# Latent attention in a three-block transformer stack: both first maxima and exponentials of a head ahead of its divides, and the next head's key copied behind the fourth divide

## What is computed

```python
def _mla_attention(q_nope, q_rope, k_nope, k_rope, v):
    scale = (MLA_NOPE + MLA_ROPE) ** -0.5
    for blk in range(seqlen // Q_BLOCK):            # 8 blocks of 128 queries
        s = (einsum('bqhd,bkhd->bhqk', q_nope[:, q0:kend], k_nope[:, :kend])
             + einsum('bqhr,bkr->bhqk', q_rope[:, q0:kend], k_rope[:, :kend]))
        s = where(mask, s * scale, -inf)             # causal
        p = softmax(s, axis=-1)
        outs.append(einsum('bhqk,bkhd->bqhd', p, v[:, :kend]))
```

## Time and profile before

| quantity | value |
|---|---|
| median of 3 executions | 2763.44 us (2759.21 to 2766.43) |
| the profiled execution's own time | 2762.98 us |
| its span | 2761.1 us |
| busy in the span: PE, PEld | 97%, 78% |
| busy in the span: DVE, ACT, POOL | 56%, 33%, 36% |

### The profile page before, as it was taken

How to read it: one execution, slowest core, us unless ns; L and a number is a source line. 1 busy time by engine, 2 the same in 40 slices (tenths; PEclk the granted TensorE clock), 3 DMA queues, 4 the chain that set the end, 5 groups by cost and what they waited for, 6 DMA issues and landing times.

```text
span 2761.1 us, 31304 instructions
## 1 busy us (share of the span) xinstructions
PE 2687.1 (97%) x12562; PEld 2153.2 (78%) x12562; DVE 1535.0 (56%) x1724; ACT 914.3 (33%) x1166; POOL 996.2 (36%) x1038
## 2 busy tenths in 40 slices
PE   8999999999999999999999999989999999999998
PEld 7877877787887887887666777767888888888886
DVE  6636663778658658569757566674322222222266
ACT  3537870421212112113347656673211001110032
POOL 4633435431432432432422222225433333333342
PEclk9999999999999999999999999999999999999999
DMA  3110003110110110111230000002111111111212
GB/s 133 53 43 31 24 31 103 65 46 16 46 46 16 46 47 24 46 39 37 71 122 24 31 24 31 31 16 100 53 46 49 52 46 50 50 46 53 89 65 76
DMA packets 39929, 139.31 MB, mean 50 GB/s; under 512 B 4400, under 2 KB 4528, under 8 KB 39792
## 3 DMA queue, kind: packets, MB, share of 16 engines
q1 hardware_dynamic: 31392, 110.11, 12.1%
q10 hardware_dynamic: 8400, 27.26, 2.7%
HBM read 124.77 MB, written 12.58 MB: 50 GB/s over the span
## 4 chain that ended last, share of the span: by engine, by line
PE 82%; DVE 11%; ACT 4%; issue 2%; POOL 1%; ACTq 0%; DVEq 0%; POOLq 0%
PE PS L652 62%; PE PS L889 2%; PE PS L982 2%; PE PS L1023 2%; PE PS L788 1%; PE PS L1208 1%; PE PS L1225 1%; PE PS L802 1%; PE PS L1366 1%; PE PS L1025 1%; PE PS L1247 1%; PE PS L929 1%; DVE ssd_x L2410 1%; DVE ssd_a_upto_lo L2392 1%; PE PS L1011 1%
## 5 line engine op out<-in xcount | busy, mean ns | idle before, releaser
L556 POOL CAST w_hi<-w_stage 128x1024 fp32r<-128x1024 f32 x202 | 218.0, 1079 | 1599.8 <-PE PS L652 1241.6
L559 POOL TENSOR_TENSOR w_lo<-w_stage,w_hi 128x256 fp32r<-128x256 f32 x808 | 728.3, 931 | 16.2
L652 PE MATMUL PS<-XH,w_hi 128*128 128x512 f32 x1216 | 385.0, 398 | 6.8 <-DVE XL L2329 2.8
L652 PE MATMUL PS<-XL,w_hi 128*128 128x512 f32 x1216 | 376.4, 391 | 0.0
L652 PE MATMUL PS<-XH,w_lo 128*128 128x512 f32 x1216 | 375.4, 390 | 0.0
L652 PEld LDWEIGHTS PS<-XH,w_hi 128*128 128x128 f32 x1216 | 222.8, 188 | 60.2 <-issue 9.4
L652 PEld LDWEIGHTS PS<-XL,w_hi 128*128 128x128 f32 x1216 | 228.8, 188 | 49.0
L652 PEld LDWEIGHTS PS<-XH,w_lo 128*128 128x128 f32 x1216 | 228.7, 188 | 48.8
L1988 ACT ACTIVATE ffn_t<-ffn_t 128x1024 f32<-128x1024 f32 x32 | 33.9, 1060 | 530.7 <-DVE ffn_t L2761 530.7
L652 PE MATMUL PS<-raw_hi,w_hi 128*128 128x512 f32 x608 | 188.0, 390 | 0.0
L652 PE MATMUL PS<-raw_hi,w_lo 128*128 128x512 f32 x608 | 187.2, 389 | 0.0
(11 more groups left out here) (421 smaller groups left out, 4914.4 us busy)
## 6 DMA issues: line engine op xcount, KB each, us to landing
w_stage<-w SPq DMA_DIRECT2D x202, 512.0 KB, 3.3
H<-x_t ACTq DMA_DIRECT2D x8, 512.0 KB, 8.2
pj_kept<-ple_proj_tiles ACTq DMA_DIRECT2D x8, 512.0 KB, 2.6
h_kept<-H ACTq DMA_DIRECT2D x8, 512.0 KB, 3.4
H<-h_kept ACTq DMA_DIRECT2D x4, 1024.0 KB, 4.9
out_t<-out_tiles SPq DMA_DIRECT2D x16, 256.0 KB, 2.1
x_again<-x_t ACTq DMA_DIRECT2D x12, 256.0 KB, 3.1
ple_proj_a<-pj_kept ACTq DMA_DIRECT2D x1, 2048.0 KB, 8.1
```

The source lines that it names most:

```text
L556: nc.gpsimd.tensor_copy(w_hi[:, slot, :, :], w_stage[:, slot, :, :]).then_inc(s_w_hi, 1)
L559: nc.gpsimd.tensor_tensor(w_lo[:, slot, k:k + 2, :], w_stage[:, slot, k:k + 2, :], w_hi[:, slot, k:k + 2, :].bitcast(F32), ALU.subtract).t ...
L652: mm = nc.tensor.matmul(outs[:, half, :], wt[:, slot, k, :], a[:, k - first, half * HB:(half + 1) * HB], start=(k == whole[0] and wt is w_ ...
```

## The change

Nothing is added or taken away. On ACT, `divide(u, 0)` moves behind `exponentials(u, 1)`, and `k_hi(u + 1)` behind `divide(u, 3)` and `chunk_hi(u, 3)`. On DVE, `neg_max(u, 1)` and chunk 9's low part of the head before come ahead of `invert(u, 0)` and `add_low(u - 1, 1)`, and `k_lo(u + 1)` comes behind `chunk_lo(u, 3)`. PE, POOL and SP keep their order.

```diff
@@ ACT, in the loop over heads
                 exponentials(u, 0)
                 if u == 0:
                     gated_hi(1)
-                divide(u, 0)
                 if u:
                     chunk_hi(u - 1, 9)
                 exponentials(u, 1)
+                divide(u, 0)
                 divide(u, 1)
                 if u:
                     low_part(u - 1, 0)
...
                 exponentials(u, 3)
                 chunk_hi(u, 2)
                 divide(u, 2)
+                divide(u, 3)
+                chunk_hi(u, 3)
                 if more:
                     k_hi(u + 1)
-                divide(u, 3)
-                chunk_hi(u, 3)
                 exponentials(u, 4)
@@ DVE, in the loop over heads
                 neg_max(u, 0)
-                if u:
-                    add_low(u - 1, 1)
-                invert(u, 0)
                 neg_max(u, 1)
                 if u:
                     chunk_lo(u - 1, 9)
+                invert(u, 0)
+                if u:
+                    add_low(u - 1, 1)
                 invert(u, 1)
...
                 invert(u, 3)
                 neg_max(u, 4)
+                chunk_lo(u, 3)
                 if more:
                     k_lo(u + 1)
-                chunk_lo(u, 3)
                 neg_max(u, 5)
```

## The result

The changed kernel takes 2783.71 us (median of 4 executions, 2778.96 to 2791.33), the kernel before 2761.32 (4 executions, 2758.92 to 2766.43). The ratio is 1.0082, with a 95% interval of 1.0067 to 1.0098. The change makes the kernel slower by 22 us; 2773 was forecast, with a range from 2766 to 2780.

What follows compares the result with a forecast made beforehand. PE was taken to bound the kernel, so time changes only where PE stands still or starts later. From 2763.0 us, +8.3 (key copy), -1.4 (last head) and +3.5 (clock) gave 2773.4, said as 2773 us, range 2766 to 2780.

Steps and rivals of the forecast that it cites:

- What bounds the kernel, and where the change acts: PE, busy 2687.1 of 2761.1 us, sets the time; the weight loads' 1.6 us of short waits for k_lo decide.
- The key copy, +8.3 us: Heads 0 to 6: k_lo and so row 5's scores come 1.19 us later, 7 x 1.19 = +8.3 us.
- The first rows, nothing in heads 0 to 6: Second maximum and exponential come 1.1 us earlier on DVE and ACT, but PE gains nothing, covered by the query products.
- The last head, -1.4 us: PE's 2.37 us wait for chunk 9's low part shrinks by 1.1 to 1.2, perhaps 0.5 more from the clock: -1.4 us.
- TensorE's clock, +3.5 us: Longer PE waits before the value projection in heads 0 to 6 bring two to three more clock falls at 1.4: +3.5 us.
- falls in nearly every head: Rival: six more clock falls at 1.65 us in heads 0 to 6, 2779.8 us in all; chance 0.15.
- the page's 0: By the Trainium skill's page, which warns only of longer idle gaps, the clock term is 0 and the time 2770.
- the row of 2.37 us: Profile row of PE's wait for chunk 9's low part in head 7, followed by a clock fall; cited against the page.

Runs made afterwards that it cites:

- first_rows_only: Only the first half of the change (both maxima and exponentials ahead of the first divide, chunk 9's split earlier), against the kernel before: 2760.63 us, ratio 0.9995.
- third_divide_ahead: First half of the change kept, second not; divide(u, 2) ahead of exponentials(u, 3), its inverse ahead of neg_max(u, 3), k_lo ahead of neg_max(u, 4): 2759.27 us.
- the key's three variants: Kernel before with only the second half of the change (2795.44 us), only ACT's part of that (2790.48 us), or only DVE's part (2799.03 us).
- key_only: Kernel before with only the second half of the change, k_hi behind divide(u, 3) and chunk_hi(u, 3), k_lo behind chunk_lo(u, 3): 2795.44 us, ratio 1.0109.

## Why the prediction was wrong, step by step

**What bounds the kernel, and where the change acts: right.** The short wait for `k_lo` in the earlier trace rows was the one that decided, and the long one for the divides was not.

**The key copy, +8.3 us: right, in mechanism and size.** `k_lo` 1.19 us later was forecast; heads at full clock are 1.23 longer. Over the seven heads, the windows from 211.43 to 406.21 take 194.78 us; before, the first maxima of heads 0 and 7 stand at 212.73 and 388.42, so that 175.69 passed, 19.1 less. Six heads at 26.03 in place of 24.80 and head 0 with 26.36 in place of 25.55 make 6 x 1.23 + 0.81 = 8.2 of this. The kernels with filled waits have heads of 26.0 from head 1 to 6 and nothing else.

**The first rows, nothing in heads 0 to 6: right** for the middle heads (24.81 us in the kernel with this half alone); head 0 gained 0.3 (25.25 against 25.55), the few tenths that were allowed for. **The last head, -1.4 us: near in size, wrong in its parts.** The wait did fall from 2.37 to 1.17, but not 1.1 to 1.2 us came of it: at full clock in both orders the head is 0.52 shorter, since PE then waits 0.77 for the second divide, which the prediction named without taking it off. The clock was put at 0.5 and gave 1.26. In `first_rows_only` the sum is 1.78 and in the changed kernel 1.87, just beyond the bound of 1.7. That the two errors nearly cancel is luck, and where the clock falls in head 7 all the same, as in `third_divide_ahead`, the head takes 26.33 in place of 26.58. In the total the half is worth 0.5 us with an interval from 3.9 less to 1.1 more, which contains the forecast, and no gain as well.

**TensorE's clock, +3.5 us: here the prediction failed.** The term was named, but its price and its bounds were too small. It went: "between two and three more at 1.4", each "at most half of 3.3 = 1.65". In the profiled execution the falls cost 2 x 1.55 + 2 x 4.56 = 12.2 us in heads 2, 3, 5 and 6, from 27.6 and 30.60 less 26.04; the one fall of before cost 1.3; so 10.9 more. With 8.2 of lateness that is the 19.1 us above; 1.9 come off in head 7 and 1.3 ahead of head 0, where nothing was changed and one fall of the kernel before is missing by chance, and 15.9 of the 16.0 us are found. So the number of falls was forecast well, three more in heads 0 to 6 of this execution; what failed is the price of one, 3.0 us in the mean. The median lies 4.7 us above the profiled execution, and the three longer executions have a lower mean clock (0.987 to 0.991 against 0.993); that their surplus is falls too is argued from the clock alone, since none of them has a trace.

The wrong step was to take the cost of a fall from the only one that the trace of before had in these heads, and the bound from its length. A fall behind the long wait need not last 3.4 us: in heads 5 and 6 it lasts 10.2. Where in the head it begins goes with its length. In the six profiled executions with a wait of 1.4 to 1.9 us in heads 0 to 6 (the changed kernel twice, the key's three variants, the wide products), the 9 falls that began 15.6 to 16.1 us behind the head's first maximum lasted 3.4 us, and the 18 that began 16.3 to 17.2 behind it lasted 10.2 or 13.7. The value projection is in the long ones whole, and eight of its narrow products take 1.90 us instead of 1.06. That these keep the clock low is a reading that fits the lengths; the run with wide products between the narrow ones was meant to try it, but its three falls all began where falls are short anyway, so it stays open. What is shown is that the falls are the 15 us: with two or six more products in the wait, the lateness unchanged to 0.1 us a head, they are gone, and so are 15 us.

The same error sat in the rivals. The largest of them, falls in nearly every head, was put at 2780; `key_only`, whose profiled execution has long falls in six of seven heads, took 2795.

The Trainium skill ("TensorE: Matmul & The Clock Gate", section "Why this matters for your kernels") was cited rightly: the idle gaps that it warns of are longer than this one. The trace does not agree: behind waits of 1.88 us the clock fell in four of seven heads, and this cost more than the lateness. The prediction had set the page's 0 aside on the row of 2.37 us, and the measurement bears that out.

## What to carry to other kernels

A short wait in the list of waits is not always a small matter: it can mark a result that is only just late. Here the 1.19 us put ahead of such a result were paid in full, while the longer wait in front of it was worth nothing. Before an instruction is moved behind others, look for who is released by its successor on the next engine. Where PE stands still close to narrow products, count with the clock as a second price, take its size from the longest stay at the low level that could follow, and try two extra products in the gap before giving up on an order.

## What the runs showed of the hardware

- By the clock record of the traces, a stay at the low level in heads 0 to 6 lasted 3.4, 6.8, 10.2 or 13.7 us. In `key_only` the long stays come back each time: heads 2 to 6 take 30.56 to 30.61 us, one like the other.
- Two extra products of 128x512 in a wait of 1.9 us, 0.5 us of work, took the changed kernel from 2784 to 2769.
- The same instructions behind the attention, which no kernel here changes, took 2346.10 us in the profiled execution of before, 2346.08 in that of the changed kernel and 2350.45 in that of `third_divide_ahead`; the clock is 0.91 in a stretch there where it was 1.00 before:

```profile
1470.00:1510.00 40.00, 36.43 (x163) 27.49 (x162) 30.33 (x29) 26.16 (x30) 10.76 (x10) 0.91 0.09 27
408.15:2758.60 2350.45, 2296.49 (x10427) 1829.43 (x10425) 1283.03 (x1375) 667.11 (x775) 816.70 (x878) 0.99 0.15 50
```

```profile
1477.00:1517.00 40.00, 36.45 (x173) 27.63 (x173) 31.09 (x29) 28.58 (x30) 10.71 (x10) 1.00 0.09 27
415.00:2761.10 2346.10, 2293.16 (x10427) 1826.81 (x10425) 1283.47 (x1375) 666.87 (x775) 817.52 (x878) 1.00 0.15 50
```

  Ten of the fourteen profiled executions took 2345.6 to 2346.3 us there, three took 2350.5 or 2350.6, one 2347.5. Nothing shows that the edit decides which: the executions of `third_divide_ahead` alone fall into two groups, 5 us apart in the mean. A difference of 4 us between two single executions can thus come from a stage that the edit doesn't touch, and it is as much as this last edit was worth.
